# The last token tile's low parts: a subtraction on TensorE and a copy on ScalarE in place of a VectorE subtraction

## The reference, cut to what matters

```python
for l in range(DEPTH):                       # DEPTH = 2
    ...                                      # mixer, x = x + gate * mixer(h)
    hp = modulate(xp, norm_ffn[l], mp[3], mp[4])
    hs = modulate(xs, norm_ffn[l], ms[3], ms[4])
    xp = xp + mp[5] * hier_moe(hp, router_g_w[l], ...)
    xs = xs + ms[5] * hier_moe(hs, router_g_w[l], ...)

def hier_moe(h, wg, bg, we, be, w1, w3, w2):
    # top-1 of 4 groups, then top-2 of its 4 experts, their softmax weights
    comb = ...                               # (tokens, 16)
    a = silu(x @ w1[e]) * (x @ w3[e]) * comb[:, e]
    return sum over e of a @ w2[e]
```

## Time and profile before

| | us |
|---|---|
| median of 3 runs (lowest, highest) | 771.26 (770.49, 771.87) |
| the profiled execution | 771.06 |
| its span, first to last instruction | 769.2 |
| PE busy in the span | 749.6 |
| DVE busy | 393.5 |
| ACT busy | 173.2 |
| mean granted TensorE clock | 0.996 |

### The profile page before, as it was taken

One profiled execution on the slowest core, in us unless ns is written; L12 is line 12 of the kernel. 1 busy time (PEld: TensorE's weight loads), 2 busy tenths in 40 slices (PEclk: granted clock), 3 DMA queues, 4 the chain that ended last, 5 costly groups with the idle time before them and its releaser, 6 DMA issues.

```text
span 769.2 us, 9951 instructions
## 1 busy us (share of the span) xinstructions
PE 749.6 (97%) x3877; PEld 370.1 (48%) x3877; DVE 393.5 (51%) x844; ACT 173.2 (23%) x431; POOL 2.4 (0%) x12
## 2 busy tenths in 40 slices
PE   7999999998999999999998999998999999999997
PEld 3364546445544434534445658445545345444434
DVE  2216177947535336326337996636633454345326
ACT  4111574035310110110116103025311101110111
POOL 0000000000000000000000000000000000000000
PEclk9999999999999999999999999999999999999999
DMA  8979995268999999999999968056699999999994
GB/s 341 426 221 431 426 430 216 109 265 354 419 404 420 430 424 427 429 427 423 424 415 428 428 250 328 3 216 251 251 377 424 426 425 429 428 429 426 423 415 188
DMA packets 32850, 277.05 MB, mean 360 GB/s; under 512 B 7789, under 2 KB 8833, under 8 KB 12833
## 3 DMA queue, kind: packets, MB, share of 16 engines
q1 hardware_dynamic: 32305, 274.97, 86.5%
q10 hardware_dynamic: 432, 1.28, 0.5%
q0 software_dynamic: 64, 0.13, 0.0%
HBM read 274.66 MB, written 1.70 MB: 359 GB/s over the span
## 4 chain that ended last, share of the span: by engine, by line
PE 90%; DVE 3%; DMA 3%; ACT 2%; issue 1%; SPq 1%; DVEq 0%; ACTq 0%
PE bank L2146 29%; PE bank L2171 15%; PE bank L2011 11%; PE bank L2177 6%; PE bank L2125 6%; PE bank L2571 5%; PE bank L2445 4%; PE bank L1935 3%; DMA ring<-in_ada_w 3%; PE bank L2406 2%; PE bank L2157 1%; PE bank L2152 1%; PE bank L2497 1%; PE bank L2518 1%; PE bank L2100 1%
## 5 line engine op out<-in xcount | busy, mean ns | idle before, releaser
L2146 PE MATMUL bank<-ring,Z 128*64 128x512 f32 x1024 | 226.5, 594 | 0.0
L2146 PEld LDWEIGHTS bank<-ring,Z 128*64 128x64 f32 x1024 | 71.8, 137 | 137.6 <-issue 135.6
L2171 PE MATMUL bank<-ring,Z 128*64 128x512 f32 (+1 forms) x544 | 113.9, 570 | 0.0
L2011 PE MATMUL bank<-ring,T 128*128 128x512 f32 x192 | 83.6, 593 | 0.4 <-issue 0.4
L1620 DVE TENSOR_TENSOR Z<-Z,bank 128x512 f32<-128x512 f32 x16 | 11.0, 688 | 119.4 <-PE bank L2146 119.4
L2171 PEld LDWEIGHTS bank<-ring,Z 128*64 128x64 f32 x544 | 37.5, 137 | 68.3 <-issue 66.2
L1449 DVE SCALAR_TENSOR_TENSOR Z<-ring,cond,Z 128x512 f32<-128x512 f32 x84 | 59.3, 748 | 2.5
L2011 PEld LDWEIGHTS bank<-ring,T 128*128 128x128 f32 x192 | 36.0, 190 | 44.5 <-issue 44.5
L1614 DVE COPY Z<-bank 128x512 f32<-128x512 f32 x24 | 16.6, 692 | 73.2 <-PE bank L2125 73.2
L2177 PE MATMUL bank<-ys,Cs 128*128 128x512 f32 (+1 forms) x204 | 52.2, 391 | 1.1 <-DVE ys L1637 1.1
L1650 DVE TENSOR_TENSOR x<-x,bank 128x512 f32<-128x512 f32 x84 | 52.1, 682 | 0.3
(11 more groups left out here) (242 smaller groups left out, 738.1 us busy)
## 6 DMA issues: line engine op xcount, KB each, us to landing
ring<-in_moe_w SPq DMA_DIRECT2D x62, 2048.0 KB, 14.9
ring<-in_moe_w SPq DMA_DIRECT2D x60, 1024.0 KB, 10.3
ring<-in_ada_w SPq DMA_DIRECT2D x23, 2048.0 KB, 18.3
ring<-in_moe_w SPq DMA_DIRECT2D x16, 512.0 KB, 19.3
ring<-in_a_w_out SPq DMA_DIRECT2D x2, 2048.0 KB, 15.8
ring<-in_f_w_in SPq DMA_DIRECT2D x2, 2048.0 KB, 25.5
ring<-in_f_w_out SPq DMA_DIRECT2D x2, 2048.0 KB, 19.3
ring<-in_ada_w SPq DMA_DIRECT2D x2, 1024.0 KB, 7.8
```

Source lines behind the costliest of these rows:

```text
L2011: last = pe.matmul(b[:, :], T[:, k, i * P:(i + 1) * P], w[:, k, :], start=(k == 0), stop=(k == KT - 1))
L2146: last = pe.matmul(out[BLK * u:BLK * (u + 1), :], xT[:, b, k, s0 + BLK * u:s0 + BLK * (u + 1)], w[:, k, :], start=(k == 0), stop=(k == KT ...
L2171: last = pe.matmul(out, aT[:, k, BLK * u:BLK * (u + 1)], down_columns(w2, k, a, e), start=(k == 0), stop=(k == FC - 1), skip_group_check=True)
```

## The change

The low parts of the last tile are made by PE and ACT. After each half was turned (`last_tokens`), and ACT has copied its high part out, PE adds the product of a negated identity matrix, `minus_ident`, with the high part into the same bank (`low_tokens`: one product of 512 columns for the first half, two of 256 for the second), so that the bank holds the low part; ACT copies that out in `low_out`. DVE's `low_part(l, NT - 1)` goes, for both layers. DVE fills `minus_ident` once, in layer 0. The gate copies of ACT (`gate_out`) are split so that the second `low_out` stands between two of them. The wait in `first_gather` is on `act_emptied` now. Layer 1's `busy(3)` and its function go.

```diff
@@ plan, route
-        t.fill(("tokens", l, 2, 0), "dve", bank=last_tile[0])
+        t.fill(("tokens", l, 2, 0), "act", bank=last_tile[0])
...
-        t.fill(("tokens", l, 2, 1), "dve", bank=last_tile[1])
+        t.fill(("tokens", l, 2, 1), "act", bank=last_tile[1])
         t.fill(("ada", n + 1), "dve", bank=others[1])
+        t.empty(("tokens", l, 2, 0))
         t.add(("gate", n, 0), "act", bank=others[0])
+        t.empty(("tokens", l, 2, 1))
...
-        for h in range(2):
-            t.empty(("tokens", l, 2, h))
@@ ScalarE
+            def low_out(l, hh):
+                b = stage_bank(("tokens", l, NT - 1, hh), act)
+                act.wait_ge(low_full, 2 * l + hh + 1)
+                cs = slice(HALF * hh, HALF * (hh + 1))
+                emptied_inc(act.activation(h_low[:, NT - 1, cs], b[:, :], ACT.Copy))
...
                 high_part(l, 2)
                 n = LAST_GATE[l]
+                low_out(l, 0)
                 ada_product(n + 1)
-                ada_read(n)
+                gate_out(n, 0)
+                low_out(l, 1)
+                gate_out(n, 1)
@@ VectorE
                 dve.wait_ge(act_emptied, turn[("gate", MIX_GATE[l] + 1, 1)][3])
+                if l == 0:
+                    dve.tensor_scalar(minus_ident[:, :], ident, -1.0, None, ALU.mult)
...
                 one_hot(pairs[l], QUAD)
-                low_part(l, NT - 1)
@@ TensorE
+            def last_tokens(l, hh):
+
+                b = begin(("tokens", l, NT - 1, hh))
+                for q in range(4):
+                    last = pe.matmul(b[:, q * P:(q + 1) * P], T[:, 4 * hh + q, (NT - 1) * P:NT * P], ident,
+                                     start=(q == 0), stop=True, is_transpose=True, skip_group_check=True)
+                last.then_inc(full, 1)
+
+            def low_tokens(l, hh):
+                b = banks[turn[("tokens", l, NT - 1, hh)][0]]
+                pe.wait_ge(h_high_out, 2 * NT * l + 2 * (NT - 1) + hh + 1)
+                for a, e in high_pieces(NT - 1, hh):
+                    last = pe.matmul(b[:, a - HALF * hh:e - HALF * hh], minus_ident[:, :], high(NT - 1, a, e),
+                                     start=False, stop=True, skip_group_check=True)
+                last.then_inc(low_full, 1)
...
-                tokens_half(l, NT - 1, 1)
+                last_tokens(l, 1)
+                low_tokens(l, 0)
                 n = LAST_GATE[l]
                 ada_product(n + 1)
+                low_tokens(l, 1)
                 done_by(("ada", n))
                 gate_read(n, 0)
...
                 if l == 0:
                     ada_product(20)
-                else:
-                    busy(3)
@@ first_gather
-                                pe.wait_ge(dve_emptied, turn[("tokens", l, NT - 1, 1)][3])
+                                pe.wait_ge(act_emptied, turn[("tokens", l, NT - 1, 1)][3])
```

More of the change, by code:

```diff
@@ L601, in build @@
         ssq, rsq = small[:, 96:126], small[:, 128:158]
+        minus_ident = sb_over("minus_ident", [P, P], F32R, "small")
         PC = sb("PC", [P, NH, P])
@@ L792, in build @@
         h_high_out = sem("h_high_out")
+        low_full = sem("low_full")
         normed = sem("normed")
@@ L1073, in ada_product, with gate_out @@
                 emptied_inc(act.activation(ada_row[:, ROW_OF[n], :], b[:, :], ACT.Copy))
-            def ada_read(n):
[L1076 to L1081, removed]
-                    for k in range(2):
-                        b = stage_bank(("gate", n, k), act)
-                        emptied_inc(act.activation(gate_b[:, k, HALF * (cc % 2):HALF * (cc % 2 + 1)], b[:, :], ACT.Copy))
+            def gate_out(n, k):
+                l, cc = ADA[n]
+                s = 2 * l + (cc >= 10)
+                if k == 0 and s > 0:
+                    act.wait_ge(x_ready, NT * s)
+                b = stage_bank(("gate", n, k), act)
+                emptied_inc(act.activation(gate_b[:, k, HALF * (cc % 2):HALF * (cc % 2 + 1)], b[:, :], ACT.Copy))
+            def ada_read(n):
+                if ADA[n][1] in GATE_CHUNKS:
+                    for k in range(2):
+                        gate_out(n, k)
+            def low_out(l, hh):
[3 more added lines that the diff above has]
+                emptied_inc(act.activation(h_low[:, NT - 1, cs], b[:, :], ACT.Copy))
             def ada(n0, n1):
@@ L2048, in route @@
                 last.then_inc(full, 1)
-                tokens_half(l, NT - 1, 0)
+                last_tokens(l, 0)
                 done_by(("logits", l))
@@ L2076, in route @@
                     ada_product(20)
-                else:
-                    busy(3)
-            def busy(n):
-                for _ in range(n):
-                    pe.matmul(banks[7][:, 0:2 * P], ident, cst[:, 0:2 * P], start=True, stop=True)
             def moe(l):
```

## The result

The changed kernel takes 772.96 us (median of 14 runs, 770.77 to 774.27), the kernel before 771.12 (14 runs, 770.07 to 771.87): ratio 1.0023, 95% interval 1.0015 to 1.0030, so 1.8 us slower. The forecast of 771.1, with a range of 770.6 to 771.8 for itself and up to 772.5 in 8 of 10 cases, was wrong. The profiled execution took 772.63 us, its span 770.8 at a mean clock of 0.997.

What follows compares the result with a forecast made beforehand. PE, busy 97% of the span, was taken as the bound. Profiled 771.06 us, +0.28 for layer 0, -0.3 for layer 1, gave 771.04; said as 771.1 since the runs' median was 0.2 higher. Range 770.6 to 771.8; 8 in 10: 769.8 to 772.5.

Steps and rivals of the forecast that it cites:

- the path up to the rank products: Both routers: added PE products delay the rank products, by 0.28 us in layer 0 and 0.47 in layer 1.
- the low parts held up nothing: Layer 1's gather: low parts ready over 1 us before product 15 reads them, so taking them off DVE removes no wait.
- Rival 2: Both layers: low parts were the last wait, so the full 1.35 us comes off each; 768.4 us, chance 0.05.
- at work without a gap from there; so its whole chain moves by 0.47: Layer 1's router: DVE works without a gap after the rank products, so gate row and gate reads move by 0.47 us.
- I take the middle, -0.3 us: Layer 1 up to the experts: half-clock stretch placed between two positions, -0.7 and about 0; bounds -1.4 and +1.3 us.
- The third rival: PE in layer 1, 538 to about 545 us: clock stays low twice as long; 772.2 to 773.3 us, chance 0.12.
- The rule named with it: PE's clock: keep TensorE continuously busy or it is halved; speaks against removing the unread products, giving the third rival's time.

Runs made afterwards that it cites:

- e11: The kernel before, unaltered, measured against itself: 771.61 us, ratio 1.0007.
- e5: The kernel before with layer 1's three unread products moved ahead of the last two gate reads, into PE's idle time: 770.13 us against 771.42, ratio 0.9986.
- e2: The changed kernel with the three unread products put back ahead of layer 1's gather: 772.67 us, ratio 1.0018 to the kernel before.
- e15: The kernel before with the change in layer 0 only, unread products kept, measured a second time: 771.39 us, ratio 1.0013.
- e16: The changed kernel with two more writes of the negated identity on VectorE in layer 0: 772.11 us against 771.49 of before, ratio 1.0009.
- e1: The kernel before without layer 1's three unread products, subtraction still on VectorE: 771.56 us against 771.32, ratio 1.0006.
- e9: The changed kernel with layer 0's subtracting products and ScalarE copies moved off the path, behind the gate reads: 771.81 us against 771.27 of before, ratio 1.0016.
- e6: The kernel before with the three added products alone, unread, in both layers: 771.23 us, ratio 1.0001.
- e7: The kernel before with the change in layer 0 only, unread products kept: 772.24 us, ratio 1.0009.
- e8: The kernel before with the change in layer 1 only, unread products kept: 771.87 us, ratio 1.0006.
- e13: The kernel before with the change in layer 0 only, ScalarE's two copies moved behind the gate copies: 772.24 us against 770.72, ratio 1.0016.
- e14: The kernel before with the change in layer 0 only, subtracting products and ScalarE copies both off the path: 772.00 us, ratio 1.0020.
- e18: The changed kernel measured once more, unaltered: 772.88 us, ratio 1.0017 to the kernel before.
- e12: The changed kernel measured again, unaltered: 772.04 us, ratio 1.0018 to the kernel before.
- e4: The changed kernel with subtracting products and ScalarE copies moved later, in layer 1 into PE's idle time with two unread products: 770.28 us, ratio 0.9986 to before.
- e17: The late-products kernel with two unread products (e4), plus two more negated-identity writes on VectorE in layer 0: 770.02 us, ratio 0.9983 to before.
- e10: The changed kernel with layer 1's three subtracting products and two ScalarE copies moved into PE's idle time: 771.67 us, ratio 1.0011 to before.

## Why the prediction was wrong

**Right: the path up to the rank products.** Layer 0 was to lose 0.28 and lost 0.29 (20.62 to 20.91); layer 1 0.47 and lost 0.46 (19.61 to 20.07), by one fp32r product of 512 columns and two of 256 in each. No gather product waits for ScalarE's copies, they hide in its idle time, and no transfer was added. That the low parts held up nothing was right for the profiled execution only: where the clock stayed up (e11, e5) they held the gather some 0.3 us, and e2 against e15, both with the unread products, the stop and no half clock, shows that gained (7.86 against 8.21). Rival 2, the full 1.35 us in both layers, is out.

**Wrong: "at work without a gap from there; so its whole chain moves by 0.47".** VectorE's chain from the rank products to the gate row moved by 0.47 and got 0.34 longer (2.71 to 3.05), by a stop of 0.44 us. All 14 traces whose layer 0 subtraction is off VectorE have one in this router and none of the 6 others has; that it comes from VectorE's program being shorter fits e16 but is not shown. It was in no term and no rival. It can't be seen in the trace of before, but that trace does have stops of this kind elsewhere.

**Wrong: "I take the middle, -0.3 us", for the clock.** This term was to hold all of layer 1: the 0.47 of added products, the unread products taken out, the gather and its clock. In the traces it measured (20.07 + 9.39) - (19.61 + 8.53) = +1.3 us (the means are worked out below), the bound that was given as +1.3; the third rival itself goes to +2.0, so the term's bound was set too low. What failed is that the unread products were weighed against a single execution with half clock.

Three traces of the changed kernel have 8.48, 9.73 and 9.96 us from the rank products to the experts; those of before 9.03 and 7.83. What separates them is the half clock: one stretch, two, two; one, none. Of the six traces whose layer 1 router lacks the unread products and has its long idle time unfilled (the changed kernel's three, e1, e9, e16), three have two stretches; of the nine with unread products in their old place (before, e11, e2, e6, e7, e8, e13, e14, e15) none has. e18 shows that the fill of the stretch ahead doesn't decide it alone: 3.08 of 3.40 us of work and a second stretch, where the changed kernel's first trace had 3.08 and none.

By the mean clock of an execution: 0.995 or less in 10 of 37 executions of the changed kernel (its own, e12's and e18's), whose median is 773.39 us, and in 2 of the 165 of before whose clock is on record; 0.998 or more in 8 of 37 (median 771.88), and in 68 of 165 (770.45). The mean counts stretches only roughly, as the clock is also low behind the last products (from 766.7 us to the end in before): 0.996 went with one stretch in the traces of before and e7 and with two in e1, e12 and e18. The seven traces with 0.997 all have one. At that value the changed kernel's median is 772.28 us (9 executions) and that of before 771.52 (46): at an equal clock it is some 0.8 us slower, about what the added products cost, and the rest of the difference goes with more and longer stretches; nine executions are few, so this is a rough division.

The third rival, which gave 772.2 to 773.3 and had a chance of 0.12, is what happens in a good part of the executions. The rule named with it, the Trainium skill, "TensorE: Matmul & The Clock Gate", section "Why this matters for your kernels", is borne out in part: with the idle time filled the clock did not fall in e4, e5 and e17, but the page speaks of idle gaps longer than any here (the longest single wait of TensorE at this router is 1.65 us in the changed kernel), so it did not foretell this fall, and e11 against before shows the same spacing with and without one. Its section "Part 1: The HAM clock gate" says that the number of slow products differs between executions; e11 against before shows that with 1.2 us (7.83, 9.03).

**The sum, done again.** By the whole of the path, before is 637.09 with a stretch and 636.10 without; with the shares of their mean clocks, 95 and 68 of 165, that makes 636.7. The changed kernel's three traces have a mean of 638.6, a difference of 1.9 us, beside 1.8 measured (1.0015 to 1.0030, so 1.2 to 2.3). Of it 0.75 are the added products (0.29 + 0.46), 0.13 waits for weights (0.4 in one of three), and about 0.9 lie between the rank products and the experts: (8.48 + 9.73 + 9.96) / 3 = 9.39, against 0.58 x 9.03 + 0.42 x 7.83 = 8.53. The stop is in that 0.9. The remaining 0.2 is in the pieces not shown. Three traces are few, and they are slow ones: their executions took 772.63, 773.25 and 774.22 us, on average 0.6 more than all 37 (772.76), while before has a mean of 771.25, so 1.5 less. The agreement to 0.1 is luck; the delays of 0.29 and 0.46 and the stop are the same in each trace.

**Open.** How much of the 0.9 is the stop and how much the clock, since a later gate read also shifts where the half clock falls. Why e2, with the unread products back, is still 1.4 over before and in 2 of 10 executions at a mean clock of 0.995; why e6 shows none of its 0.7 us, and e14 1.5 (0.5 to 2.5) where its trace gives some 0.5: with a dozen runs and a kernel that reads 0.5 us off against itself, terms of this size can't be told by time, only by trace. And whether the waits for weights, 0.4 to 0.8 us in e2, e7, e10, e16 and e18, belong to the change: e15, the same kernel as e7, has none, but all five are among the ten traces with 20.9 us in the column of layer 0, and the ten with 20.6 have none. So layer 0's products on the path may bring them in about half of the executions, which would be some 0.3 us on average; no run tested this by itself.

## What to carry to other kernels

Cost an edit on the bounding engine from several executions, not one: where the clock can fall in an idle stretch, each kernel has a spread of such stretches, and an edit also changes their share. If unread products are to keep the clock up, they belong into the idle time itself, ahead of the operation that is waited for (e4, e5, e17: 0.14 to 0.17% faster than before, mean clock 0.998 or more in all 33 executions), not behind it on the path. And when instructions leave an engine's program, look for stops marked "issue" before and after: they move with the program, and may land on the path.

## What the runs showed of the hardware

- TensorE's clock fell to half in stretches of 3.41 or 6.83 us, behind a stretch of 3.4 us in which it had been busy for 1.1 to 1.7 us, and in some executions of the same program it did not fall. It can stay low through a second stretch in which TensorE is busy for all of 3.40 us (e1 from 541.50, e12 from 542.90, e18 from 543.70). In these three the stretch ahead held 2.80, 2.46 and 3.08 us of work; in before and in the changed kernel's first trace it held 3.15 and 3.08, and the clock came back.
- VectorE stands still for 0.42 to 0.46 us at a few places, with nothing that it waits for in the rows. Such places are the same in two executions of one program (the changed kernel's first trace and e12); two writes added in layer 0 moved those behind them, the one in layer 1's router by two rows (e16).
- Three products with a constant, 256 columns of fp32, ahead of a gate read that waits anyway, left its start where it was (2.70 us behind the rank products in e5, 2.71 before), and the kernel was 1.1 us faster than with them behind it (ratio 0.9986); behind it they took 1.1 us at full clock (539.34 to 540.44 in e11).
